# Two LayerNorm stages behind the experts: scale and bias moved out of the rows

## What is computed

```python
def _post_norm(x, sub, g, b):
    return _layer_norm(DN_ALPHA * x + sub, g, b)      # alpha = (2*DEPTH)**0.25

for l in range(DEPTH):
    ...                                               # mixer (l = 0: GLA and SSD, l = 1: pooling and MoBA)
    xp = _post_norm(xp, mp, ln_g[l, 0], ln_b[l, 0])
    xp = _post_norm(xp, _hier_moe(xp, *moe), ln_g[l, 1], ln_b[l, 1])
```

## Time and profile before

| | |
|---|---|
| time, median of 3 runs | 1364.89 us (1362.83 to 1367.19) |
| the profiled execution's own time | 1365.28 us |
| its span, first to last instruction | 1363.7 us |
| PE busy, share of the span | 82% |
| DVE busy | 36% |
| ACT busy | 18% |
| Pool busy | 14% |
| moved from and to HBM | 276 GB/s over the span |
| mean granted TensorE clock | 0.909 of full speed |
| granted clock in n10's tiles, 950 to 1010 | 1.00 in every stretch of 10 us |
| n01, first issue to the next stage's first | 622.54 to 667.56 |
| n10, first issue to the next stage's first matmul | 943.14 to 1044.36 |
| n11, first issue to the end of the last vector instruction | 1319.91 to 1360.47 |

### The profile page before, as it was taken

One profiled execution on the slowest core, in us unless ns is written; L12 is line 12 of the kernel. 1 busy time (PEld: TensorE's weight loads), 2 busy tenths in 40 slices (PEclk: granted clock), 3 DMA queues, 4 the chain that ended last, 5 costly groups with the idle time before them and its releaser, 6 DMA issues. The chain is left out here.

```text
span 1363.7 us, 15222 instructions
## 1 busy us (share of the span) xinstructions
PE 1118.1 (82%) x5745; PEld 568.7 (42%) x5745; DVE 484.8 (36%) x1308; ACT 249.3 (18%) x529; POOL 193.9 (14%) x184
## 2 busy tenths in 40 slices
PE   7999999969799787780699898988997998777540
PEld 5864666635543222220343344545555332222110
DVE  3515665466711111104412323644665111111017
ACT  0311232311111111111311212241221111111012
POOL 0000000000011111003334542220001111111022
PEclk9999998989899898895699998987998999888785
DMA  7520301291679999967576997882915999999623
GB/s 261 188 73 1 128 1 62 70 370 78 224 272 421 421 419 421 421 268 271 212 296 240 374 357 281 308 325 100 393 63 220 392 418 420 420 421 423 292 104 139
DMA packets 84851, 360.41 MB, mean 264 GB/s; under 512 B 13858, under 2 KB 18083, under 8 KB 54819
## 3 DMA queue, kind: packets, MB, share of 16 engines
q1 hardware_dynamic: 62882, 280.67, 51.7%
q0 software_dynamic: 19808, 74.48, 14.3%
q10 hardware_dynamic: 2080, 4.19, 0.8%
HBM read 344.90 MB, written 31.16 MB: 276 GB/s over the span
## 5 line engine op out<-in xcount | busy, mean ns | idle before, releaser
L1692 PE MATMUL e_psum_g<-m_wg,top_xT 128*64 128x512 f32 x736 | 185.2, 652 | 55.9 <-DMA m_wg<-in_moe_w_gate_up 53.2
L1692 PEld LDWEIGHTS e_psum_g<-m_wg,top_xT 128*64 128x64 f32 x736 | 56.7, 150 | 176.9 <-issue 111.2
L1716 PE MATMUL e_psum_y<-m_wd,top_xT 128*64 128x512 f32 x528 | 123.4, 610 | 5.4 <-DMA m_wd<-in_moe_w_down 3.4
L1280 PE MATMUL ahead_psum<-top_wide,top_xT 128*128 128x512 f32 x240 | 111.0, 609 | 8.6 <-DVE top_X L1397 8.6
L1746 DVE COPY top_xT<-e_psum_x 128x512 f32<-128x512 f32 x33 | 22.8, 692 | 211.8 <-PE e_psum_x L1677 211.8
L1183 POOL DMA_INDIRECT m_xg<-token_rows,m_tokof x33 | 33.5, 1016 | 431.0 <-PE e_psum_x L1677 241.6
L1692 PE MATMUL e_psum_g<-top_wide,top_xT 128*64 128x512 f32 x320 | 78.3, 635 | 17.2 <-DMA top_wide<-in_moe_w_gate_up 17.2
L1988 PE MATMUL cd_psum_ab<-top_wide,top_xT 128*128 128x512 f32 x192 | 85.4, 598 | 0.0
L1832 POOL DMA_INDIRECT cd_kv<-in_cache_kT,top_kpages x64 | 62.0, 968 | 90.1 <-PE cd_psum_d L2030 44.6
L1755 DVE TENSOR_SCALAR e_Y<-e_psum_y,m_share 128x512 f32<-128x512 f32 x33 | 24.8, 751 | 130.5 <-PE e_psum_y L1716 130.5
L1280 PEld LDWEIGHTS ahead_psum<-top_wide,top_xT 128*128 128x128 f32 x240 | 44.6, 194 | 55.9 <-issue 55.8
(11 more groups left out here) (465 smaller groups left out, 1632.2 us busy)
## 6 DMA issues: line engine op xcount, KB each, us to landing
m_wg<-in_moe_w_gate_up SPq DMA_DIRECT2D x88, 1024.0 KB, 25.9
m_wd<-in_moe_w_down SPq DMA_DIRECT2D x64, 1024.0 KB, 25.6
top_wide<-in_moe_w_gate_up SPq DMA_DIRECT2D x40, 1024.0 KB, 24.8
cd_kv<-in_cache_kT SPq DMA_DIRECT2D x64, 256.0 KB, 6.2
m_wg<-expert_rows SPq DMA_DIRECT2D x16, 512.0 KB, 7.3
ab_w<-in_ab_w_in SPq DMA_DIRECT2D x2, 2048.0 KB, 11.7
top_wide<-in_ab_w_in SPq DMA_DIRECT2D x2, 2048.0 KB, 7.9
top_wide<-in_ab_w_out SPq DMA_DIRECT2D x2, 2048.0 KB, 7.9
```

The costliest lines, as they stand in the source:

```text
L1280: last = nc.tensor.matmul(pp[(2 * i + h) % 3][:P, :], mixT[:, k, tok0(t):tok0(t) + P], w[h][:, k, :], start=(k == 0), stop=(k == KD - 1))
L1692: last = nc.tensor.matmul(pg[i % 2][64 * a:64 * a + 64, :], xgT[i % 2][:, j, 64 * a:64 * a + 64], wg[2 * (i % NR) + a][:, j * 512:(j + 1) ...
L1716: last = nc.tensor.matmul(py[n2][64 * a:64 * a + 64, :], hT[:, j, 64 * a:64 * a + 64], wd[2 * (i % NR) + a][:, j * D + n2 * 512:j * D + (n ...
```

## The change

It touches the two combining stages, the end of the expert stages and the settle stage of layer 1.

1. **Early rows.** SP, at the end of `expert_stage`, waits until Pool reports that all scatters have landed and then asks for the two results of the first two tiles of the order, before all engines meet. The combining stages ask only for the other three tiles.
2. **Pool held.** Pool's add of tile i now waits until DVE has done `add(i-1)`.
3. **n01, now `pass_stage`.** The rows are normalised only, and stored so. g and b are loaded with features on partitions (`gbT`, 16 numbers on each partition) and applied when the transposed blocks are copied to `xT`: block by block, six blocks by ACT and two by DVE (four and four for the last tile), from six PSUM buffers instead of two. `affine` is gone.
4. **n10.** The rows read back lack g and b of the LayerNorm before. They are loaded by four broadcast DMAs into the two `xg` buffers, right behind the first row tile in SP's queue, and DVE's new `restore(i)` applies them in two instructions ahead of `affine(i-1)`; alpha is folded in. Pool's clearing of `xg` waits for the last `restore`. For the first tile `prepare_out` runs between the two adds, and PE projects the whole of `project(1, 0)` ahead of `flip(0)`.
5. **n11, now `final_stage`.** g and b are loaded as one line each and spread over the partitions by four matmuls with ones into PSUM, from where `affine` reads them. DVE's order is `add(i)`, `scale(i)`, `affine(i-1)`. The last tile skips ACT: (x - mean)·g, then times 1/root plus b.

```diff
-def combine_stage(nc, name, C, X, lng, lnb, y_dram, E, then=None, xT=None, rows=None, out=None):
+def combine_rows(E):
+    return [w[:, 0:2 * D].rearrange("p (k n) -> p k n", k=2) for w in E.wg[0:4] + E.wd[0:1]]
...
+def load_rows(sp, y, y_dram, y_in, tiles):
+    for t, P in tiles:
+        for k in range(2):
+            row = ROWS * k + tok0(t)
+            sp.dma_start(y[t][:P, k, :], y_dram[row:row + P, :]).then_inc(y_in[t], 16)
...
+def pair_rows(nc, pool, y, y_in, added, paired):
+    for i, (t, P) in enumerate(ORDER):
+        pool.wait_ge(y_in[t], 32)
+        if i >= 1:
+            pool.wait_ge(added, i)
+        nc.gpsimd.tensor_tensor(y[t][:P, 0, :], y[t][:P, 0, :], y[t][:P, 1, :], ALU.add).then_inc(paired, 1)
...
+def sum_and_spread(nc, V, dve, c, X, y, i, t, P, st, mv, rstd, paired, added, var_in):
+    x = X[:P, t, :]
+    dve.wait_ge(paired, i + 1)
+    V.scalar_tensor_tensor(out=x, in0=x, scalar=ALPHA, in1=y[t][:P, 0, :], op0=ALU.mult, op1=ALU.add).then_inc(added, 1)
+    dve.wait_ge(added, i + 1)
+    for h in range(2):
+        c.add(V.bn_stats(st[:P, t, h, :], x[:, h * 512:(h + 1) * 512]))
+    c.wait()
+    c.step(V.bn_aggr(mv[:P, t, :], st[:P, t, :, :].rearrange("p a b -> p (a b)")))
+    V.tensor_scalar(rstd[:P, t:t + 1], mv[:P, t, 1:2], LN_EPS, None, ALU.add).then_inc(var_in, 1)
...
+def pass_stage(nc, name, C, X, ln_T, y_dram, E, then, xT, rows):
...
-        gb = s.sb("gb", [128, 2, D])
...
-        y = [w[:, 0:2 * D].rearrange("p (k n) -> p k n", k=2) for w in E.wg[0:4] + E.wd[0:1]]
...
+        gbT = s.sb("gbT", [128, 2, KD])
+        y = combine_rows(E)
+        pt = [s.ps(f"t{i}") for i in range(6)]
...
+        def turned(i, k):
+            P, bank = ORDER[i][1], (0, 0, 0, 0, 1, 1, 2, 2)[k]
+            at = k - (0, 4, 6)[bank]
+            return pt[3 * (i % 2) + bank][:, at * P:(at + 1) * P]
+        def copy_chunk(eng, i, k):
+            t, P = ORDER[i]
+            dst, src = xT[:, k, tok0(t):tok0(t) + P], turned(i, k)
+            g, b = gbT[:, 0, k:k + 1], gbT[:, 1, k:k + 1]
+            if eng is nc.scalar:
+                return nc.scalar.activation(dst, src, ACT.Identity, bias=b, scale=g)
+            return nc.vector.tensor_scalar(dst, src, g, b, ALU.mult, ALU.add)
...
         @block.sync
         def _(sp):
-            for t, P in ORDER:
-                for k in range(2):
-                    row = ROWS * k + tok0(t)
-                    sp.dma_start(y[t][:P, k, :], y_dram[row:row + P, :]).then_inc(y_in[t], 16)
-            sp.dma_start(gb[:, 0, :], lng.partition_broadcast(128)).then_inc(gb_in, 16)
-            sp.dma_start(gb[:, 1, :], lnb.partition_broadcast(128)).then_inc(gb_in, 16)
...
+            load_rows(sp, y, y_dram, y_in, ORDER[2:])
+            sp.dma_start(gbT[:, :, :], ln_T).then_inc(gb_in, 16)
...
             for i, (t, P) in enumerate(ORDER):
-                sp.wait_ge(final, i + 1)
...
+                sp.wait_ge(normed, i + 1)
+                sp.dma_start(rows[tok0(t):tok0(t) + P, :], X[:P, t, :]).then_inc(stored, 16)
...
         def _(pool):
-            for t, P in ORDER:
-                pool.wait_ge(y_in[t], 32)
-                nc.gpsimd.tensor_tensor(y[t][:P, 0, :], y[t][:P, 0, :], y[t][:P, 1, :], ALU.add).then_inc(paired, 1)
...
+            pair_rows(nc, pool, y, y_in, added, paired)
...
+        @block.tensor
+        def _(pe):
+            for i, (t, P) in enumerate(ORDER):
+                pe.wait_ge(normed, i + 1)
+                if i >= 2:
+                    pe.wait_ge(T_act, i - 1)
+                    pe.wait_ge(T_dve, i - 1)
+                for k in range(KD):
+                    last = nc.tensor.transpose(turned(i, k), X[:P, t, k * 128:(k + 1) * 128], C("ident")[:P, :P])
+                last.then_inc(T_in, 1)
...
             for i in range(6):
                 if i < 5:
-                    add(i, *ORDER[i])
+                    t, P = ORDER[i]
+                    sum_and_spread(nc, V, dve, c, X, y, i, t, P, st, mv, rstd, paired, added, var_in)
+                    dve.wait_ge(root, i + 1)
+                    c.step(V.reciprocal(rstd[:P, t:t + 1], rstd[:P, t:t + 1]))
+                    V.tensor_scalar(nmr[:P, t:t + 1], mv[:P, t, 0:1], rstd[:P, t:t + 1], -1.0, ALU.mult, ALU.mult)\
+                     .then_inc(mean_in, 1)
                 if i >= 1:
-                    affine(i - 1, *ORDER[i - 1])
-                if i < 5:
-                    scale(i, *ORDER[i])
+                    if i == 1:
+                        dve.wait_ge(gb_in, 16)
+                    dve.wait_ge(T_in, i)
+                    for k in range(6 if i < 5 else 4, KD):
+                        last = copy_chunk(V, i - 1, k)
+                    last.then_inc(T_dve, 1)
...
-                if xT is not None and i >= 1:
-                    t, P = ORDER[i - 1]
+                if i >= 1:
+                    if i == 1:
+                        act.wait_ge(gb_in, 16)
                     act.wait_ge(T_in, i)
-                    for h in range(2):
-                        last = nc.scalar.activation(xT[:, 4 * h:4 * h + 4, tok0(t):tok0(t) + P],
-                                                    pt[h][:, :4 * P].rearrange("p (c n) -> p c n", c=4), ACT.Copy)
-                    last.then_inc(T_out, 1)
+                    for k in range(6 if i < 5 else 4):
+                        last = copy_chunk(nc.scalar, i - 1, k)
+                    last.then_inc(T_act, 1)
...
+def final_stage(nc, name, C, X, lng, lnb, y_dram, E, out):
...
+        line = E.wd[1][0:1, 0:2 * D]
+        g, b = s.ps("g", 2 * 512), s.ps("b", 2 * 512)
...
+        @block.sync
+        def _(sp):
+            sp.dma_start(line[:, 0:D], lng.partition_broadcast(1)).then_inc(line_in, 16)
+            sp.dma_start(line[:, D:2 * D], lnb.partition_broadcast(1)).then_inc(line_in, 16)
+            load_rows(sp, y, y_dram, y_in, ORDER[2:])
...
+        @block.tensor
+        def _(pe):
+            pe.wait_ge(line_in, 32)
+            for h in range(4):
+                last = nc.tensor.matmul((g, b)[h // 2][:, 512 * (h % 2):512 * (h % 2) + 512], C("ones")[0:1, :],
+                                        line[:, 512 * h:512 * h + 512], start=True, stop=True)
+            last.then_inc(gb_out, 1)
...
+            def affine(i, t, P):
+                dve.wait_ge(normed, i + 1)
+                if i == 0:
+                    dve.wait_ge(gb_out, 1)
+                c.step(V.tensor_tensor(X[:P, t, :], X[:P, t, :], g[:P, :], ALU.mult))
+                V.tensor_tensor(X[:P, t, :], X[:P, t, :], b[:P, :], ALU.add).then_inc(final, 1)
+            def last_tile(i, t, P):
+                x = X[:P, t, :]
+                c.step(V.scalar_tensor_tensor(out=x, in0=x, scalar=mv[:P, t, 0:1], in1=g[:P, :], op0=ALU.subtract, op1=ALU.mult))
+                dve.wait_ge(root, i + 1)
+                c.step(V.reciprocal(rstd[:P, t:t + 1], rstd[:P, t:t + 1]))
+                V.scalar_tensor_tensor(out=x, in0=x, scalar=rstd[:P, t:t + 1], in1=b[:P, :], op0=ALU.mult, op1=ALU.add)\
+                 .then_inc(final, 1)
+            for i, (t, P) in enumerate(ORDER):
+                sum_and_spread(nc, V, dve, c, X, y, i, t, P, st, mv, rstd, paired, added, var_in)
+                if i < 4:
+                    scale(i, t, P)
+                if i >= 1:
+                    affine(i - 1, *ORDER[i - 1])
+            last_tile(4, *ORDER[4])
...
+        @block.scalar
+        def _(act):
+            for i, (t, P) in enumerate(ORDER):
+                act.wait_ge(var_in, i + 1)
+                nc.scalar.activation(rstd[:P, t:t + 1], rstd[:P, t:t + 1], ACT.Sqrt).then_inc(root, 1)
+                if i == 4:
+                    break
...
             if back:
-                for t, P in ORDER:
+                for i, (t, P) in enumerate(ORDER):
                     sp.dma_start(X[:P, t, :], back(t)).then_inc(x_in[t], 16)
+                    if i == 0:
+                        for p, got in ((slice(0, 32), old_in), (slice(32, 128), rest_in)):
+                            for a in range(2):
+                                sp.dma_start(E.xg[a][p, :], old[a].partition_broadcast(p.stop - p.start)).then_inc(got, 16)
...
         @block.gpsimd
         def _(pool):
+            if old:
+                pool.wait_ge(old_used, 1)
             for x in E.xg:
                 nc.gpsimd.memset(x[:, :], 0.0).then_inc(blank, 1)
...
             for i in range(1, 5):
-                project(i, 0, first)
+                project(i, 0, full if old and i == 1 else first)
                 if done == 3 and i == 1:
                     project(1, 1, first)
                     prepare()
                 flip(i - 1, 0)
                 flip(i - 1, 1)
-                project(i, 0, second)
+                if not old or i > 1:
+                    project(i, 0, second)
...
+            def restore(i):
+                t, P = ORDER[i]
+                dve.wait_ge(x_in[t], 16)
+                if i <= 1:
```

(57 more changed lines are left out.)

82 lines of the change are left out of this document (35 added, 47 removed).

## The result

The changed kernel takes 1353.23 us, median of 5 runs (1351.35 to 1356.52), beside 1367.19 for the kernel before (1362.83 to 1368.96): ratio 0.9891, 95% interval 0.9869 to 0.9912. It is faster, by 14 us. Two later comparisons of the same two kernels gave 0.9891 (0.9859 to 0.9924) and 0.9853 (0.9820 to 0.9885). The profiled execution took 1351.45 us with a span of 1349.7.

What follows compares the result with a forecast made beforehand. It took waits stage by stage: DVE paces n01 and n11, PE bounds n10. Terms -14.0 (n01), +3.0 (n10) and -6.0 (n11) sum to -17.0 on 1365.28, giving 1348.3 us, range 1344 to 1355.

Steps and rivals of the forecast that it cites:

- Early rows: n01 and n11: asking for rows early saves the way through the stage's start, 0.9 us each, bounds 0 and 2.3.
- One tile of DVE: n01: one tile takes DVE 4.0 us in place of 5.6, with ACT, PE and Pool hidden.
- The wait for g and b: n01: DVE waits 1.2 us for gbT, landing at 636.0; bounds 634.75 (no wait) and 640.2.
- A wait above 3 us: n01: sign that the forecast is wrong, if DVE waits for gbT for more than 3 us.
- PE idle once, before the second transposes of tile 1,: n10: restoring stalls PE for 2.5 us at this one place, stage +3.0; later tiles absorb it in waits.
- The clock after the stall: n10, rival, chance 0.06: PE's clock falls after the 2.5 us stall, losing 3.2 us; time 1351.5.
- gbT is late: n01, rival, chance 0.10: gbT lands near 640.2, so n01 gives only -9.8; time 1352.5.
- The broadcasts cost nothing: n10: the four broadcasts (1.05 MB) delay nothing, as nothing behind them is needed before 960.
- Pool's clearing: n10: Pool's two clearings beside DVE's affine(3) cost 0, bounds 0 and 1.5 us.
- restore on the path in every tile: n10, rival, chance 0.07: restoring costs 12.5 us in place of 3.0; time 1357.8.
- n10 hides it all: n10, rival, chance 0.08: the restoring costs no time there; time 1345.3.
- the slower rival: n10, rival, chance 0.02: broadcasts into xg run one after another, costing 22 us; time 1370.3.

Runs made afterwards that it cites:

- e10: Changed kernel without the two products that restore each tile in n10: 1493.11 us, with 24 scatters instead of 17 in layer 1's experts.
- e6: Changed kernel with all rows asked for in the combining stages, none from the expert stages: 1357.01 us, 0.9929 of the kernel before.
- e9: The kernel before, unchanged, profiled a second time: 1373.80 us, ratio 0.999 to before.
- e7: Changed kernel without Pool's wait for DVE's add: 1349.20 us, 0.9866 of the kernel before.
- e4: Changed kernel with the second half of tile 2's product moved ahead of tile 1's second transposes on PE: 1348.35 us, 0.9836 of the kernel before.
- e11: Changed kernel again, unaltered, in more rounds: 1354.37 us.
- e8: Changed kernel with the edits of e4 and e5 together: 1341.07 us, 0.9820 of the kernel before.
- e12: Same kernel as e8, in more rounds: 1348.39 us, 0.9817 of the kernel before.
- e1: Changed kernel again, unaltered, for its second profile: 1357.15 us.
- e5: Changed kernel with gbT asked for ahead of n01's six row transfers: 1346.68 us, 0.9865 of the kernel before.

## Why the prediction was right

Forecast 1348.3 on the first profile's time, range 1344 to 1355; measured 1353.23, inside that range but outside the forecast's own 1345.5 to 1351. By the stages it was -17.0 forecast and -16.1 measured. That these two are so close is luck in part: errors of about 2 us, told below, cancelled.

**n01, forecast -14.0:** -13.0 (50.8 to 37.8 in the mean of three). *Early rows* were mis-sized: 0.9, and the first add came 1.9 to 2.3 us nearer to the scatter. *One tile of DVE:* 4.0, measured 4.2; the two copies take 0.72 and not 0.48. *The wait for g and b:* 1.2, measured 3.36, 2.76 and 2.47. Counted from the last scatter, which stood 0.75 us earlier in this profile, DVE was ready 0.9 us before the forecast and `gbT` landed 1.2 us after it (20.5 and not 19.3; in the two later profiles 19.5 and 19.3). The early rows' surplus thus bought little in n01. A wait above 3 us was named as a sign that the forecast was wrong: the first profile shows it, the other two don't, and the term is mis-sized by 1.3 to 2.2 us. The next stage comes 0.7 to 0.8 us after the last copies, as 0.9 said.

**n10, forecast +3.0:** +4.1 to the last transposes and +0.8 in the tables. *PE idle once, before the second transposes of tile 1,* 2.5 forecast, 2.97 measured; all later tiles took the restoring into their waits. *The clock after the stall* was a rival with 0.06; it came in six of seven profiles and cost 1.0 to 2.5 us, where the rival had 3.2. Its chance was set too low for what the earlier trace rows already showed. The rivals' 1351.5 (this one) and 1352.5 (*gbT is late*) are both nearer to the time measured than the forecast; only the first of the two happened. *The broadcasts cost nothing* is right for the sum, but by cover only: e10 shows the wait of 1.95 behind them once the restoring is gone. And the 2.5 us of the stall, put down to `restore(1)` alone, came out right partly by luck, since 2.37 us of it are there without any restoring. One reading behind this was wrong: the 6.2 us of the earlier trace rows, taken for n10's, is a median over the settle stages of both layers. In n10 of the kernel before the pair landed later (KB, us from issue to landing):

```profile
m_wd<-in_ln_g SPq DMA_DIRECT2D x1, 512.0 KB, 8.0
m_wd<-in_ln_b SPq DMA_DIRECT2D x1, 512.0 KB, 9.1
```

*Pool's clearing:* 0, right. Both MEMSETs run from 1002.67 for 1.84 us, and `affine(3)` beside them has its 0.69 as ever (DVE's timeline of the changed kernel):

```profile
1003.24 0.69 DVE L1555 TENSOR_TENSOR top_X<-top_X,m_wd 128x512 f32<-128x512 f32 x1
```

The Trainium skill (SBUF — State Buffer, Who interferes with whom) said so for a GpSimd instruction that only writes, and the trace agrees. The tables have two lengths, 24.7 to 25.2 and 26.3 to 26.6. The three profiles with the old n10 are all of the short kind, those of the table with the new one are four short and six long. The lengths go with two groups of filler products (`idle_products`), the first at 3.27 or 4.95 us, the second between 3.72 and 6.56, over stretches granted anything from 0.50 to 1.00. Whether the 0.8 belong to the change stays open.

**n11, forecast -6.0:** -8.0, outside its bounds of -4.1 and -7.4. *Early rows* again: 0.9, measured 3.4 (first add 12.45 after the scatter before, 9.00 after; e6 12.49). My upper bound of 2.3 supposed that half of the time from scatter to request was landing. The request now leaves 3.3 us after the scatter, where it left 6.6 after, so half of it was the way through the stage's start. What follows was as written: second add 1.2 and not 3.30, tile 5.94, PE's spread 0.17 late, `affine` from PSUM 1.21, 29.9 to 30.3 us from first add to the end (forecast 29.45; before 34.5 and 34.8).

The 3.30 us of the second add are easily read as 2.1 us that the hold of Pool saved. They are not: in e9, the same kernel, that add took 1.20, and n11 was as long (47.07 and 47.14), because DVE then waited longer for the broadcast b. DVE's timeline before, then in e9:

```profile
1336.52 1.79 DVE L255 TENSOR_TENSOR top_X<-top_X,n_gb 32x1024 f32<-32x1024 f32 x1 [2.03 <-DMA n_gb<-in_ln_b]
```

```profile
1340.55 1.20 DVE L236 SCALAR_TENSOR_TENSOR top_X<-top_X,m_wg 128x1024 f32<-128x1024 f32 x1
...
1348.29 1.35 DVE L255 TENSOR_TENSOR top_X<-top_X,n_gb 32x1024 f32<-32x1024 f32 x1 [4.78 <-DMA n_gb<-in_ln_b]
```

From first to third add n11 took 13.9 and 14.1 us before and takes 9.95 to 10.4 now, as there is no wait for g and b; the short last tile gives another 1.4, and the longer tiles take 0.7 back. The hold pays only once that wait is gone: then e7 shows its 2.1 us as 2.3.

So the mis-sized terms, early rows (2.5 more in n11, 1.2 more in n01) and the clock behind the stall with the tables (-1.9), nearly cancelled, which nothing in the forecast foresaw, and the wait for `gbT` took n01's part back. *gbT is late* to 640.2 and *restore on the path in every tile* did not happen; *n10 hides it all* did not as it stands, and nearly does with e4's order (0.6 us over the kernel before). The four broadcasts into `xg` were issued within 1.4 us and landed 3.2, 3.3, 5.2 and 7.9 us later, so they did not run one after another: the slower rival fell.

## What to carry to other kernels

When a stage is made faster at its head, look at once for the small transfer that stands last in its queue: here 8 KB behind ten transfers of rows took back what the earlier rows had gained, and putting them first cost nothing that a row shows. Where a vector-engine step is added ahead of TensorE's transposes, put a piece of the next product into the gap in the same edit; the gap costs its own length and then, in six of seven profiles here, the clock. And when a slow instruction is seen beside another engine's work, look at what its engine waits for next: the 2.1 us of the slow add in n11 only shortened the wait behind it. Judge such edits by the stage's own length in two or three profiles: stretches that nobody touched moved by up to 7 us between profiles of one kernel, more than most of these edits are worth.

## What the runs showed of the hardware

- A stall of 2.97 us in full work at clock 1.00 was followed in six of seven profiles by eight products at 4.6 to 6.2 us in place of 3.60; the seventh (e11) had the same stall and a granted clock of 1.00 behind it. One of 0.5 us (e4, e8, e12) or 2.37 us (e10) was not followed by slower products.
- Beside Pool's adds the DVE instruction with two SBUF inputs took 3.37 us for 1.22, the same width with one input in PSUM 1.21, and statistics of one input their usual 1.29 for two (e7). Pool's own add took 3.07 for 2.34 once. Reading g and b from PSUM therefore also frees `affine` of Pool; with g in SBUF the product beside Pool's last add took 1.79 us in n11 of the kernel before.
- The last scatter of layer 0, before anything changed has run but for its own stage's end, stood at 615.9 to 623.7 us, 616.68 and 623.65 for the kernel before itself; and a stall of ACT of 3 to 5 us in layer 1's mixer appears in all four profiles of e1 to e4 and of e9 to e12 and in none of e5 to e8.
